# Value projection directly behind the rope key's; the query latent's spread between its halves; the last two recurrent norms behind it

## The reference, cut to what matters

```python
cq, ckv_raw, kr_raw, hq, hf, hi, hg, cu, cv, ga, gb, gc = jnp.split(x @ lw['w_in'], idx, axis=-1)
cq = rms_norm(cq, lw['q_norm_g'])            # query latent, 256 wide
q = (cq @ lw['w_uq']).reshape(...)           # 8 heads
ckv = rms_norm(ckv_raw, lw['kv_norm_g'])     # key/value latent, 256 wide
krope = rope(kr_raw[:, :, None], pos)        # rope key, 32 wide
...                                          # recurrence: o_h, S_fin
y_a = jnp.einsum('bshr,rhv->bshv', o_lat, lw['w_uv']).reshape(...) @ lw['w_pa']
o_h = rms_norm(o_h, lw['hg_norm_g'])         # one norm per token and recurrent head
y_b = (o_h * jax.nn.silu(hg)) @ lw['w_pb']
m = sig(ga)*y_a + sig(gb)*y_b + sig(gc)*y_c
```

## Time and profile before

| | us |
|---|---|
| median of 3 runs | 1983.66 (1983.3 to 1984.87) |
| the profiled execution's own time | 1983.82 |
| its span, first to last instruction | 1982.0 |
| TensorE busy, matmuls | 1955.4 (99%) |
| TensorE busy, weight loads | 1871.6 (94%) |
| VectorE busy | 1358.5 (69%) |
| ScalarE busy | 883.5 (45%) |
| GpSimd busy | 81.6 (4%) |

### The profile page before, as it was taken

One profiled execution on the slowest core, in us unless ns is written; L12 is line 12 of the kernel. 1 busy time (PEld: TensorE's weight loads), 2 busy tenths in 40 slices (PEclk: granted clock), 3 DMA queues, 4 the chain that ended last, 5 costly groups with the idle time before them and its releaser, 6 DMA issues.

```text
span 1982.0 us, 42425 instructions
## 1 busy us (share of the span) xinstructions
PE 1955.4 (99%) x17562; PEld 1871.6 (94%) x17562; DVE 1358.5 (69%) x2247; ACT 883.5 (45%) x1580; POOL 81.6 (4%) x96
## 2 busy tenths in 40 slices
PE   7999999999999999999999999999999999999999
PEld 6899998898999999999988999989889999999998
DVE  5588646774379998863468976477725899889433
ACT  4364235444345555553355532354433454556322
POOL 1000001000011000000010000010000200000100
PEclk9999999999999999999999999999999999999999
DMA  5223213222132233333332232132203222333321
GB/s 180 75 72 91 77 42 105 61 60 54 54 106 77 75 107 107 91 97 90 93 93 75 81 91 69 45 99 62 70 28 99 88 86 76 107 104 97 89 88 54
DMA packets 287935, 164.25 MB, mean 83 GB/s; under 512 B 8985, under 2 KB 279553, under 8 KB 287745
## 3 DMA queue, kind: packets, MB, share of 16 engines
q1 hardware_dynamic: 283712, 152.07, 27.1%
q0 software_dynamic: 3552, 8.36, 1.4%
q10 hardware_dynamic: 480, 1.13, 0.2%
HBM read 156.86 MB, written 4.66 MB: 81 GB/s over the span
## 4 chain that ended last, share of the span: by engine, by line
PE 95%; DVE 3%; issue 1%; ACT 1%; DMA 0%; DVEq 0%; ACTq 0%
PE acc L873 47%; PE ring L1297 13%; PE acc L859 7%; PE acc L1267 6%; PE ring L897 4%; PE acc L1297 3%; PE ring L1150 2%; PE ring L1169 1%; PE acc L897 1%; PE ring L1158 1%; PE ring L1220 1%; PE ring L1202 1%; PE ring L1515 1%; DVE wlo L2401 1%; DVE xf L2401 0%
## 5 line engine op out<-in xcount | busy, mean ns | idle before, releaser
L2401 DVE TENSOR_TENSOR wlo<-raw,whi 128x1024 fp32r<-128x1024 f32 (+2 forms) x372 | 326.2, 884 | 290.9 <-ACT whi L1641 290.0
L1641 ACT ACTIVATE whi<-raw 128x512 fp32r<-128x512 f32 (+1 forms) x371 | 287.9, 784 | 446.4 <-PE acc L873 361.0
L873 PE MATMUL acc<-xh,whi 128*128 128x272 f32 x992 | 230.3, 313 | 3.4 <-DVE xl L2401 2.9
L873 PE MATMUL acc<-xl,whi 128*128 128x272 f32 x992 | 206.5, 289 | 0.0
L873 PE MATMUL acc<-xh,wlo 128*128 128x272 f32 x992 | 206.5, 289 | 0.0
L873 PEld LDWEIGHTS acc<-xh,whi 128*128 128x128 f32 x992 | 158.0, 191 | 19.2 <-issue 10.8
L873 PEld LDWEIGHTS acc<-xl,whi 128*128 128x128 f32 x992 | 157.6, 190 | 0.0
L873 PEld LDWEIGHTS acc<-xh,wlo 128*128 128x128 f32 x992 | 157.1, 190 | 0.0
L1297 PE MATMUL ring<-xb,whi 128*128 128x272 f32 x768 | 147.1, 289 | 2.1 <-ACT xf L1641 2.0
L873 PE MATMUL acc<-hh,whi 128*128 128x272 f32 x704 | 145.7, 288 | 0.1
L873 PE MATMUL acc<-hl,whi 128*128 128x272 f32 x704 | 145.1, 287 | 0.0
(11 more groups left out here) (510 smaller groups left out, 4605.9 us busy)
## 6 DMA issues: line engine op xcount, KB each, us to landing
raw<-in_w_in_dram SPq DMA_DIRECT2D x104, 512.0 KB, 3.7
raw<-in_w_up_dram SPq DMA_DIRECT2D x88, 512.0 KB, 3.9
raw<-in_w_down_dram SPq DMA_DIRECT2D x32, 512.0 KB, 3.9
raw<-in_w_o_dram SPq DMA_DIRECT2D x16, 512.0 KB, 3.9
raw<-in_w_down_dram SPq DMA_DIRECT2D x16, 384.0 KB, 3.3
raw<-in_w_pc_dram SPq DMA_DIRECT2D x16, 256.0 KB, 2.7
raw<-in_w_pb_dram SPq DMA_DIRECT2D x16, 256.0 KB, 2.7
raw<-in_w_pa_dram SPq DMA_DIRECT2D x16, 256.0 KB, 2.7
```

Source lines behind the costliest of these rows:

```text
L873: last = pe.matmul(dst[:, b * 512:b * 512 + HALF], w[:, c:c + P], x[:, k0 + a, b * HALF:(b + 1) * HALF], start=start and a == 0 and q == 0 ...
L1641: return act.activation(dst, src, ACT.Copy)
L2401: return dve.tensor_tensor(out, a, b, op)
```

## The change

On TensorE the first half of the value projection stands directly behind the rope key's product and takes its four banks one by one (each `group` just before its first matmul) instead of all at once. The spread of the query latent's rstd stands between the halves. The norm sums of chunk 3 go behind the second half, next to those of chunk 4; `latents_to_rows` goes ahead of `hgrn_rstd(l, 1)`, so the last two spreads stand together behind it. ScalarE's square root of chunk 3 goes behind the copies of the values, VectorE's reciprocal of chunk 3 next to that of chunk 4, and the low part of `U_MB + 1` ahead of `hgrn_scale(1)`. No instruction is added or removed; the ring's turn is now `st4`, `v0` to `v3`, `hn3`, `hn4`, `ktm0` and on.

```diff
-            latent_rstd(l, 1)
-            hgrn_sums(l, 3)
+            dsts = []
             for n in range(2):
                 unit_ready(l, U_UV + n)
                 if n == 0:
                     pe.wait_ge(*at("lat_lo", l, 1))
-                    dsts = [group(f"v{c}", l) for c in range(4)]
                 w1, w2 = whi[n % 2], wlo[n % 2]
                 for c in range(4):
+                    if n == 0:
+                        dsts.append(group(f"v{c}", l))
                     for q, (x, w) in enumerate(((ckvh, w1), (ckvl, w1), (ckvh, w2))):
                         last = pe.matmul(dsts[c][:, :], x[:, n, c * P:(c + 1) * P], w[:, 0:512], start=n == 0 and q == 0, stop=n == 1 and q == 2)
                     if n == 1 and c < 3:
                         last.then_inc(*inc("group_ready"))
                 last.then_inc(*inc("w_used"))
+                if n == 0:
+                    latent_rstd(l, 1)
             pe.wait_ge(*used_unit(l, U_UV + 1))
             pe.sem_inc(*inc("group_ready"))
+            hgrn_sums(l, 3)
             hgrn_sums(l, 4)
+            latents_to_rows(l)
             hgrn_rstd(l, 1)
-            latents_to_rows(l)
             hgrn_rstd(l, 2)
...
@@ ScalarE
             next_hi(l, U_UV + 1)
-            hgrn_std(3)
             act.wait_ge(*at("lat_done", l, 2))
             copy(cqh[:, :, :], cqn[:, :, :]).then_inc(*inc("lat_hi"))
             next_hi(l, U_MB)
             for c in range(4):
                 act.wait_ge(*group_ready(f"v{c}", l))
                 copy(vtm[:, c, :], gbank(f"v{c}")[:, :]).then_inc(*group_free(f"v{c}"))
+            hgrn_std(3)
             hgrn_std(4)
...
@@ VectorE
             next_lo(l, U_UV + 1)
-            hgrn_recip(3)
             latent(1, cqn, V_QG)
             latent_lo(1, cql, cqn, cqh)
             next_lo(l, U_MB)
...
+            hgrn_recip(3)
             hgrn_recip(4)
+            next_lo(l, U_MB + 1)
             hgrn_scale(1)
-            next_lo(l, U_MB + 1)
             hgrn_scale(2)
```

## The result

The changed kernel took 1990.26 us in the median of its first six runs (1986.87 to 1991.63) against 1982.6 us of the kernel before; the ratio is 1.0033, 95% interval 1.0022 to 1.0043. Eight more runs gave 1988.53 against 1982.63, ratio 1.0025 (1.0015 to 1.0036). The median of all fourteen is 1988.7. It is slower, as forecast (1989.1, 1986.0 to 1991.3), by 7.7 and 5.9 us in the two sets; both intervals lie above 1.

What follows compares the result with a forecast made beforehand. TensorE was taken to bound the kernel (95% of the chain that ended last). Layer 0's 2.7, layer 1's 1.1 and the clock's 1.6 sum to 5.4 us, on the median 1983.66: 1989.1 us, range 1986.0 to 1991.3.

Steps and rivals of the forecast that it cites:

- Half 0 early, a break before its last group: TensorE, layer 0: first value half starts at 314.9, idles 0.6 us before its last three matmuls; values end 1.2 us earlier.
- The latent's spread drags ScalarE's queue: Later spread delays ScalarE's latent copy to 320.95 and the value copies behind it; TensorE's norm sums stall 1.6 us.
- The query waits for low part and scaling: VectorE's low part precedes the scaling; TensorE idles 1.5 us and the query starts at 330.0, +2.7 us in layer 0.
- Layer 1 loses its old fall: Layer 1's value matmuls no longer run at low clock; query at 1299.2 against 1298.04, so +1.1 us there.
- Nothing given back: Behind the query, TensorE's waits at the scores recover nothing of the delay; at most 0.9 us in both layers.
- Clock, 0.8 per layer: New idling may lower TensorE's clock in both layers; middle of nothing and 1.6 us, so 0.8 each, 1.6 in all.
- upper end: Largest clock loss assumed: 1.6 us per layer, what the low clock cost on wide matmuls in layer 1 before.
- The sum: Both layers' delays and the clock: 2.7 + 1.1 + 1.6 = 5.4 us, so 1989.1 against the median; chance 0.53.
- Rival (a): Same chain of waits in both layers, but the clock costs nothing: +3.8 us, 1987.5; chance 0.20.
- (b): Low clock lies on the query products in both layers, 1.6 us each: +7.0 us, 1990.7; chance 0.12.
- (c): Scaling isn't held by VectorE's low part: +2.2 and +0.6 us, 1986.5 with no clock loss; chance 0.08.
- (d): Bank waits vanish and TensorE's own work sets the query at 326.5: -3.2 us in all, 1980.5; chance 0.07.

Runs made afterwards that it cites:

- the two single moves: Changed kernel, one move each: ScalarE's first query weight high part before its wait for the query latent, 1985.66 us; latent's spread behind the first half's third group, 1985.93 us.
- second look at the changed kernel: The changed kernel run again without any edit, eight more runs: median 1988.53 us, ratio 1.0025; the profiled execution was the slowest of the eight.
- head alone: Changed kernel with `latents_to_rows` put back behind `hgrn_rstd(l, 1)` and the low part of `U_MB + 1` back behind `hgrn_scale(1)`: 1988.38 us, ratio 1.0029.
- short chain: Changed kernel with the two single moves, plus VectorE's reciprocals and scalings directly behind chunk 4's gate and rope key rows between TensorE's last spreads: 1982.27 us, ratio 0.9997.
- tail alone: Kernel before with only `latents_to_rows` ahead of `hgrn_rstd(l, 1)` and the low part of `U_MB + 1` ahead of `hgrn_scale(1)`: 1986.36 us, ratio 1.0017.
- filled kernel: Changed kernel with six more matmuls of 512 columns, result unused, behind the values in TensorE's wait for the first value bank: 1987.52 us, ratio 1.0023.

## Why the prediction was right, point by point

- **Half 0 early, a break before its last group:** start 314.80, break 0.49 (predicted 314.9 and 0.6). TensorE ran 0.06 us behind the state update (317.56 to 317.62), not 0.26 as in the earlier trace rows, where it waited for all four banks at once.
- **The latent's spread drags ScalarE's queue:** copy of the latent at 320.79 (320.95), value copies from 323.12 (323.28), bank wait 1.57 (1.6). Right, and shown by the two single moves: each shortens what comes behind it.
- **The query waits for low part and scaling:** low part at 327.05 (327.4), query at 329.61, idle 1.43 (330.0, 1.5). Too late by 0.45 in the distance (16.06 against 15.61): 0.2 from the state update, the rest mostly from row copies that ran closer together (high part at 325.97, predicted 326.3). So +2.26 per layer, not +2.7.
- **Layer 1 loses its old fall:** value matmuls at full clock in the profiled run; +0.68 (15.62 - 14.94) where 1.1 was predicted, for the same 0.45. With layer 0's 2.26 that is 2.94 of the 3.05 us between the two profiled executions. The sum took that old fall for granted in the kernel before. Of the 26 runs of before that were taken beside the second set, the 7 at a mean clock of 0.997 took 1983.58 us or more, the 19 at 0.998 or 0.999 took 1983.49 or less, so most of them probably had no such fall; against those the change costs 2 x 2.26 = 4.5 us by the distances, and 4.88 between the lowest runs (1986.53 - 1981.65).
- **Nothing given back:** scores start 6.21 behind the query, as before (6.17); their wait is 0.46 as before.
- **Clock, 0.8 per layer:** the term of the sum that was mis-sized. In the profiled run it is 0, and the sign that I named for it (a window below full between 1293 and 1303 or 324 and 334) was missing there. In the second look at the changed kernel one fall cost 3.4, twice the upper end that I took from the earlier trace rows, because it lasted three times as long. Over the fourteen runs it is worth 1988.7 - 1986.9 = 1.8 us, near the 1.6 in the sum, but as a mean over runs with none and runs with a long one.
- **The sum:** 2 x 0.45 too much on the chain, and the forecast against the median of all runs is 0.4 too high. That it came so near is partly luck: the starting value of 1983.66 lay 1.1 above the medians of before that go with the two sets (1982.6 and 1982.63), the chain 0.9 too long, and the clock term was the middle of two bounds, not a mechanism that I had. The waits and their order were not luck. Rival (a), 1987.5 without a fall, is what the profiled execution showed (1986.87); (b) is near the slowest runs (1990.69 to 1991.63), and the one of them that was profiled got there by one long fall, not two of 1.6; (c) and (d) are out, since the scaling did wait for the low part, and since the bank waits didn't vanish.

Open: what decides whether a run falls, and for how long. The same wait of 1.57 us was followed by a fall in one layer of a run and not in the other, and in two profiled runs (layer 0 of the head alone and of the short chain) the clock fell near 313, ahead of every step that was moved.

## What to carry to other kernels

A step that is moved early on one engine may need a late one behind it: list what is queued behind each wait on the engines with strict order, above all copies that give PSUM banks back, and move those ahead of the wait. Several edits on one serial chain don't add; take the distance between two fixed instructions as the measure, and after each edit look which engine holds the last link. Idle time of TensorE may cost more than itself: in one profiled run a stall of 1.6 us was followed by a low clock that cost another 3.4 us, in another by none. Only the times of many runs show that, one profile doesn't.

## What the runs showed of the hardware that I had not expected

- Falls of the clock came in two lengths. Two lasted 10.2 us at half clock: that of the second look at the changed kernel, and layer 0 of the one with the low part put back (0.63, 0.50 and 0.59 in the windows from 324 to 336 us). All others near this stretch lasted some 3.4 us: layer 1 of the kernel before, the tail alone, the head alone, the short chain, and layer 1 of the one with the spread in the first half, shown here (windows, then TensorE):

```profile
1292.00:1296.00 4.00, 2.66 (x73) 1.87 (x72) 3.71 (x11) 3.85 (x14) 0.83 (x2) 0.89 0.47 155
1296.00:1300.00 4.00, 3.54 (x22) 2.90 (x20) 2.09 (x3) 2.12 (x7) 1.20 (x3) 0.68 0.33 94
```
```profile
1294.63 2.33 PE L1085 MATMUL ring<-cst,ckvn 128*128 128x128 f32 x10
...
1297.56 1.98 PE L1035 MATMUL acc<-cst,small 128*128 128x128 f32 x12
1300.57 0.49 PE L873 MATMUL acc<-cqh,whi 128*128 128x272 f32 x2 [1.03 <-DVE o L2404]
```

- Transposes alone don't make a fall long. Here (1295.1 to 1298.5) and in layer 1 of the head alone (1299.7 to 1303.0) TensorE did nothing but transposes at half clock, and full clock came back on them, before the query. In the second look at the changed kernel it did transposes without a gap from 1296.85 to 1302.63, most of them at half clock, and full clock came back only some 4 us into the query products. The Trainium skill ("TensorE: Matmul & The Clock Gate", Part 4: PE-mode transpose) says that transposes don't count as work for the full clock; the first two traces disagree, and the third alone would fit. For keeping the full clock, the filled kernel shows it through 3.4 us of transposes and 1.43 us of idling.
- A low clock makes the transposes slower, but also hides part of itself: the query's own wait was 0.61 us instead of 1.43.
- The same kernel, with the same waits, spread over 5 us from run to run; with the wait filled, over 1.8.
